# Hybrid decoder step: mixer tiles in pieces of 384, 320 and 352 tokens, weight slices laid out by parity of k

## What is computed

```
h = rmsnorm(x, g1) * (1 + scale1) + shift1;   z = h @ w_in         (mLSTM and GLA heads, gates)
y = (sigmoid(g_a) * ha + sigmoid(g_b) * hb) @ w_out;   x = x + gate1 * y
h2 = rmsnorm(x, g2) * (1 + scale2) + shift2
x = x + gate2 * ((silu(h2 @ w_gate) * (h2 @ w_up)) @ w_down)
```

## Time and profile before

| | |
|---|---|
| median of 3 runs | 1861.24 us (1857.82 to 1863.58) |
| the profiled execution, its own time | 1861.35 us |
| its span | 1859.5 us |
| TensorE matmuls | 14,443, busy 1822.0 us (98%) |
| TensorE weight loads | 14,443, busy 1741.6 us (94%) |
| VectorE, ScalarE, GpSimd busy | 57%, 37%, 39% |

### The profile page before, as it was taken

One profiled execution on the slowest core, in us unless ns is written; L12 is line 12 of the kernel. 1 busy time (PEld: TensorE's weight loads), 2 busy tenths in 40 slices (PEclk: granted clock), 3 DMA queues, 4 the chain that ended last, 5 costly groups with the idle time before them and its releaser, 6 DMA issues.

```text
span 1859.5 us, 35897 instructions
## 1 busy us (share of the span) xinstructions
PE 1822.0 (98%) x14443; PEld 1741.6 (94%) x14443; DVE 1062.4 (57%) x1886; ACT 682.3 (37%) x1401; POOL 728.6 (39%) x631
## 2 busy tenths in 40 slices
PE   7999999999999999999999999999999999999998
PEld 4899999999999999999998999989999999999998
DVE  6841645415464154541465688885675667566656
ACT  4533423334243343432435544223223223322337
POOL 4222332323333133322343773244345444544545
PEclk8999999999999999999999999999999999999999
DMA  9232222322223123222242742111112111111212
GB/s 319 103 105 57 78 86 69 118 63 82 81 69 123 53 83 90 71 87 88 83 139 84 226 120 63 46 46 47 47 46 63 29 58 58 58 35 47 69 46 94
DMA packets 182637, 154.77 MB, mean 83 GB/s; under 512 B 10325, under 2 KB 163093, under 8 KB 181961
## 3 DMA queue, kind: packets, MB, share of 16 engines
q1 hardware_dynamic: 182170, 152.27, 27.0%
q10 hardware_dynamic: 302, 0.22, 0.0%
HBM read 130.96 MB, written 21.50 MB: 82 GB/s over the span
## 4 chain that ended last, share of the span: by engine, by line
PE 83%; DVE 8%; issue 4%; POOL 2%; ACT 2%; DMA 0%; ACTq 0%; DVEq 0%; POOLq 0%; SPq 0%
PE bank L1013 28%; PE bank L2312 20%; PE bank L2281 11%; PE bank L1035 10%; PE bank L2179 2%; PE bank L1182 2%; PE bank L1184 1%; PE bank L1187 1%; PE bank L1225 1%; POOL mix L1498 1%; DVE y_rows L2926 1%; DVE x_t L2960 1%; PE bank L1160 1%; DVE y_rows L2745 1%; PE bank L339 1%
## 5 line engine op out<-in xcount | busy, mean ns | idle before, releaser
L1441 POOL TENSOR_TENSOR w_lo<-w_raw,w_hi 128x512 fp32r<-128x512 f32 x128 | 191.2, 1494 | 575.8 <-ACT w_hi L1240 575.8
L1013 PE MATMUL bank<-h_hi,w_hi 128*128 128x352 f32 x1152 | 246.7, 336 | 0.3 <-ACT w_hi L1240 0.3
L1013 PE MATMUL bank<-h_hi,w_lo 128*128 128x352 f32 x1152 | 232.6, 324 | 1.4 <-POOL w_lo L1441 1.4
L1013 PE MATMUL bank<-h_lo,w_hi 128*128 128x352 f32 x1152 | 232.1, 323 | 0.0
L2611 POOL TENSOR_TENSOR f_lo<-w_raw,f_hi 128x512 fp32r<-128x512 f32 x107 | 145.0, 1360 | 194.7 <-ACT f_hi L2376 194.7
L1013 PEld LDWEIGHTS bank<-h_hi,w_hi 128*128 128x128 f32 x1152 | 190.7, 189 | 14.6 <-issue 11.2
L2611 POOL TENSOR_TENSOR w_lo<-w_raw,w_hi 128x512 fp32r<-128x512 f32 x107 | 143.5, 1347 | 151.7 <-ACT w_hi L2376 151.7
L1013 PEld LDWEIGHTS bank<-h_hi,w_lo 128*128 128x128 f32 x1152 | 192.8, 188 | 3.7 <-POOL w_lo L1441 3.7
L1013 PEld LDWEIGHTS bank<-h_lo,w_hi 128*128 128x128 f32 x1152 | 193.2, 188 | 0.0
L2960 DVE SCALAR_TENSOR_TENSOR x_t<-bank,ada,x_t 128x352 f32<-128x352 f32 (+1 forms) x288 | 156.1, 568 | 55.5 <-PE bank L2281 38.8
L1240 ACT ACTIVATE w_hi<-w_raw 128x512 fp32r<-128x512 f32 x128 | 80.2, 626 | 107.3 <-PE bank L1013 69.8
(11 more groups left out here) (546 smaller groups left out, 4129.8 us busy)
## 6 DMA issues: line engine op xcount, KB each, us to landing
w_raw<-in_w_in SPq DMA_DIRECT2D x128, 256.0 KB, 3.0
w_ada_tile<-in_w_ada SPq DMA_DIRECT2D x32, 512.0 KB, 4.0
w_raw<-in_w_out SPq DMA_DIRECT2D x48, 256.0 KB, 2.8
w_raw<-in_w_ffn_gate SPq DMA_DIRECT2D x44, 256.0 KB, 3.0
w_raw<-in_w_ffn_up SPq DMA_DIRECT2D x44, 256.0 KB, 2.9
w_raw<-in_w_ffn_down SPq DMA_DIRECT2D x44, 256.0 KB, 2.9
w_ada_ring<-in_w_ada SPq DMA_DIRECT2D x10, 512.0 KB, 9.1
x_scratch<-x_turned_rows SPq DMA_DIRECT2D x1, 4224.0 KB, 16.3
```

The source lines that it names most:

```text
L1013: last = pe.matmul(g.ps[b][:, 0:n], x[:, s, k, :], y[:, 4 * h + k, c0:c0 + n], start=(h == 0 and k == 0 and m == 0), stop=(h == 1 and k == ...
L1441: pool.tensor_tensor(Wl[:, s], raw[:, r], Wh[:, s].bitcast(F32), ALU.subtract).then_inc(s_lo, 1)
```

## The change

1. In the mixer phase and in the first tile, the pieces of a tile are tokens 0 to 384, 384 to 704 and 704 to 1056: widths 384, 320 and 352. Their number and the sum of the widths stay. The later phase keeps 352 and 264.
2. `h_hi` and `h_lo` move by 32 bytes, so that they start at 0 mod 256.
3. The weight buffers are laid out anew. Slices with odd k lie in a second plane, 1,056 words behind that of the even ones, which is 128 mod 256. The four half buffers (high 0, high 1, low 0, low 1) lie 260 words apart, which is 16 bytes mod 256. ScalarE and GpSimd write each half as two planes of 256 words, through views of the same 512 elements.
4. For value tiles, the two column halves of one k lie next to each other in the plane of that k, so 256 columns are still streamed in one run.

With this, the distance in the mixer's `h` tiles is the same for every k: 32, 48, 64 or 80, by the half buffer that is loaded. In the value tiles it is 224, 208, 192 or 176.

```
+CUT = (0, 384, 704, T)
+ODD = 8 * P + 32
+def by_parity(w):
+    return w.rearrange("p (a b) c -> p a b c", b=2)
+def halves_of_columns(w):
+    return w.rearrange("p a b c -> p b a c")
+def slice_k(w, k):
+    return w[:, k // 2, k % 2, :]
...
         def span(c):
-            return c * PC, PC
+            return CUT[c], CUT[c + 1] - CUT[c]
...
-                        last = pe.matmul(g.ps[b][:, 0:n], x[:, s, k, :], y[:, 4 * h + k, c0:c0 + n],
+                        last = pe.matmul(g.ps[b][:, 0:n], slice_k(x[:, s], k), y[:, 4 * h + k, c0:c0 + n],
...
-                                             by_two(y[:, s])[:, k, :], start=...
+                                             y[:, s, :, k, :].rearrange("p a c -> p (a c)"), start=...
...
-                act.activation(Wh[:, s], raw[:, r], ACT.Copy).then_inc(s_hi, 1)
+                to = halves_of_columns(Wh[:, s]) if TILES[w][l][0] == "v" else Wh[:, s]
+                act.activation(to, by_parity(raw[:, r]), ACT.Copy).then_inc(s_hi, 1)
...
-                pool.tensor_tensor(Wl[:, s], raw[:, r], Wh[:, s].bitcast(F32), ALU.subtract).then_inc(s_lo, 1)
+                lo, hi = Wl[:, s], Wh[:, s]
+                if TILES[w][l][0] == "v":
+                    lo, hi = halves_of_columns(lo), halves_of_columns(hi)
+                pool.tensor_tensor(lo, by_parity(raw[:, r]), hi.bitcast(F32), ALU.subtract).then_inc(s_lo, 1)
...
-                                last = pe.matmul(g.ps[bnk][:, 0:n], x(s)[:, kk, :], y[:, 4 * h + kk, c0:c0 + n],
+                                last = pe.matmul(g.ps[bnk][:, 0:n], slice_k(x(s), kk), y[:, 4 * h + kk, c0:c0 + n],
...
-        sb("before_h", [P, 24])
+        sb("before_h", [P, 32])
...
-        sb("behind_h", [P, 8])
...
-        g.Wh = sb("w_hi", [P, 2, 4, P], F32R)
-        g.Wl = sb("w_lo", [P, 2, 4, P], F32R)
+        apart = lambda x: x[:, :, 0:4 * (2 * P + 4)].rearrange("p b (n r) -> p n b r", n=4)[:, :, :, 0:2 * P]
+        halves_at = lambda x, lo: apart(x)[:, 2 * lo:2 * lo + 2].rearrange("p s b (a c) -> p s a b c", a=2)
+        wx = sb("w_by_parity", [P, 2, ODD], F32R)
+        g.Wh, g.Wl = halves_at(wx, 0), halves_at(wx, 1)
...
-        W2 = (sb("f_hi", [P, 2, 4, P], F32R), sb("f_lo", [P, 2, 4, P], F32R))
-        g.rest = sb("rest_of_v_a", [P, NT * VX - 2 * D])
+        fx = sb("f_by_parity", [P, 2, ODD], F32R)
+        W2 = halves_at(fx, 0), halves_at(fx, 1)
+        g.rest = sb("rest_of_v_a", [P, NT * VX - 2 * ODD])
```

More of the change, by code:

```diff
@@ L267, in _ @@
                 pool.wait_ge(g.s_hi, n + 1)
-                pool.tensor_tensor(g.Wl[:, n], g.raw[:, n], g.Wh[:, n].bitcast(F32), ALU.subtract).then_inc(g.s_lo, 1)
+                pool.tensor_tensor(g.Wl[:, n], by_parity(g.raw[:, n]), g.Wh[:, n].bitcast(F32), ALU.subtract).then_inc(g.s_lo, 1)
         @block.tensor
@@ L338, in first_upper @@
                             pe.wait_ge(g.s_hsh, h + 1)
-                        pe.matmul(g.ps[c][:, 0:PC], w[:, h, k % 4, :], g.Hh[:, k, c * PC:(c + 1) * PC],
+                        pe.matmul(g.ps[c][:, 0:CUT[c + 1] - CUT[c]], slice_k(w[:, h], k % 4), g.Hh[:, k, CUT[c]:CUT[c + 1]],
                                   start=(k == 0 and m == 0), stop=False)
@@ L348, in first_lower @@
                         pe.wait_ge(g.s_hsl, h + 1)
-                    last = pe.matmul(g.ps[c][:, 0:PC], g.Wh[:, h, k % 4, :], g.Hl[:, k, c * PC:(c + 1) * PC],
+                    last = pe.matmul(g.ps[c][:, 0:CUT[c + 1] - CUT[c]], slice_k(g.Wh[:, h], k % 4), g.Hl[:, k, CUT[c]:CUT[c + 1]],
                                      start=False, stop=(k == KC - 1))
@@ L443, in weight @@
                 act.wait_ge(g.s_w[n], 48)
-                act.activation(g.Wh[:, n], g.raw[:, n], ACT.Copy).then_inc(g.s_hi, 1)
+                act.activation(g.Wh[:, n], by_parity(g.raw[:, n]), ACT.Copy).then_inc(g.s_hi, 1)
             partial(0)
@@ L784, in out_hi @@
                 act.wait_ge(s_used, MIX_HALVES + n - 3)
-            act.activation(g.W(0, out_slot(n)), raw[:, out_slot(n)], ACT.Copy).then_inc(g.f_hi, 1)
+            act.activation(g.W(0, out_slot(n)), by_parity(raw[:, out_slot(n)]), ACT.Copy).then_inc(g.f_hi, 1)
         def out_lo(pool, n):
             pool.wait_ge(g.f_hi, n + 1)
-            pool.tensor_tensor(g.W(1, out_slot(n)), raw[:, out_slot(n)], g.W(0, out_slot(n)).bitcast(F32), ALU.subtract).then_inc(g.f_lo, 1)
+            pool.tensor_tensor(g.W(1, out_slot(n)), by_parity(raw[:, out_slot(n)]), g.W(0, out_slot(n)).bitcast(F32), ALU.subtract).then_inc(g.f_lo, 1)
         def mix_hi(act, m):
@@ L1035, in mm_values @@
                             last = pe.matmul(g.ps[b][:, t % 2 * DV:(t % 2 + 1) * DV], x[:, 2 * n + k, t * P:(t + 1) * P],
-                                             by_two(y[:, s])[:, k, :], start=(n == 0 and k == 0 and m == 0 and t % 2 == 0),
+                                             y[:, s, :, k, :].rearrange("p a c -> p (a c)"), start=(n == 0 and k == 0 and m == 0 and t % 2 == 0),
                                              stop=(n == 3 and k == 1 and m == 2 and t % 2 == 1))
@@ L2228, in first_group @@
                             for kk in range(4):
-                                last = pe.matmul(g.ps[bnk][:, 0:PC], x(s)[:, kk, :], y[:, 4 * h + kk, 0:PC],
+                                last = pe.matmul(g.ps[bnk][:, 0:PC], slice_k(x(s), kk), y[:, 4 * h + kk, 0:PC],
                                                  start=(h == 0 and kk == 0 and m == 0), stop=(h == 1 and kk == 3 and m == 2))
@@ L2280, in half_piece @@
                         for m, (x, y) in enumerate(((Wh, Ah), (Wh, Al), (Wl, Ah))):
-                            last = pe.matmul(g.ps[bnk][:, 0:w], x(s)[:, r // 3, :], y[:, f, c0:c0 + w],
+                            last = pe.matmul(g.ps[bnk][:, 0:w], slice_k(x(s), r // 3), y[:, f, c0:c0 + w],
                                              start=(f == 0 and m == 0), stop=(f == 1 and m == 2))
@@ L2311, in seven @@
                             for kk in range(4):
-                                last = pe.matmul(g.ps[bnk][:, 0:HQ], x(s)[:, kk, :], BLOCK[block][kk][y][:, q * HQ:(q + 1) * HQ],
+                                last = pe.matmul(g.ps[bnk][:, 0:HQ], slice_k(x(s), kk), BLOCK[block][kk][y][:, q * HQ:(q + 1) * HQ],
                                                  start=(m == 0 and kk == 0), stop=(m == 2 and kk == 3))
@@ L2375, in hi @@
                 wait(act, s_used, n - (RING - 1))
-                act.activation(Wh(s), made_of(n), ACT.Copy).then_inc(s_hi, 1)
+                act.activation(Wh(s), by_parity(made_of(n)), ACT.Copy).then_inc(s_hi, 1)
             def t_hi(*which):
@@ L2610, in lo @@
                 wait(pool, s_used, n - (RING - 1))
-                pool.tensor_tensor(Wl(s), made_of(n), Wh(s).bitcast(F32), ALU.subtract).then_inc(s_lo, 1)
+                pool.tensor_tensor(Wl(s), by_parity(made_of(n)), Wh(s).bitcast(F32), ALU.subtract).then_inc(s_lo, 1)
             def mix_rest_lo(m):
```

## The result

The changed kernel takes 1864.49 us in the median of 22 runs (1861.72 to 1866.95), the kernel before 1861.00 us in 22 runs beside them (1857.82 to 1867.77). The ratio is 1.0021, 95% interval 1.0014 to 1.0028: slower by 0.21%, 3.5 us. By the bound of 0.3% this is "no change", by the interval a small loss. It lies in the range of 1820 to 1875, and 15 us above the forecast. The profiled execution took 1865.32 us, its span 1863.5.

The account below looks back on a forecast made before the run. It took the number of TensorE matmuls times their spacing to bound the kernel. Terms of 9.0 us (384 and 320 columns) and 3.1 (value tiles), 12.1 off 1861.35, gave 1849 us, 0.65% faster, range 1820 to 1875.

Parts of the forecast that it names:

- What bounds the kernel: Whole kernel: TensorE, busy for 98% of the span, sets the time as the number of matmuls times their spacing.
- 384 and 320 columns: Mixer `h` tiles, 2,304 matmuls: excess settles at 10.0 ns in place of 13.9, 9.0 us off.
- Value tiles: 1,536 matmuls: the tight spacing comes more often, excess 8.8 ns in place of 10.8, 3.1 us off.
- A distance that no longer alternates: Mixer and value tiles: every matmul of a run starts from what the last left; no separate size beside 9.0 and 3.1 us.
- Third pieces and the later phase: 352 pieces in mixer, output projection, plain tiles and down projection, plus seven-product tiles: other distances, counted as nothing.
- Casts and evacuations: ScalarE's cast and GpSimd's subtraction into two planes, and piece 0's later evacuation: no cost counted.
- The slower one: Rival, 352 and 256 tiles: the layout before already has the best distance; 15 us lost, 1876 us, chance 0.25.
- the classes of 264 columns: Seven-product tiles: mean excess 8.3, 11.2 or 12.5 ns by distance class, used to price the slower case.
- Its signs: For the slower case: line 1013 above 162 ns in the mean and the down projection above 161.
- No change: Rival, whole kernel: how a run begins decides its spacing, not addresses; 1861 us within 0.3%, chance 0.22.
- All tight: Rival: fixed distance alone brings tight spacing to all 352 pieces too; 66 us, 1795 to 1811 us, chance 0.11.
- The ports and the floor: Two skill rules: independent read ports, so the change does nothing; N/2.4 plus about 2.5 ns, so 352 takes 149.2 ns.

Follow-up runs that it names:

- experiment 1: Probe with TensorE alone, not a changed kernel: 32 equal matmuls for each of six lengths and 16 distances; 352 columns had 13.7 ns of excess in the mean.
- experiment 2: The kernel before with pieces of 384, 320 and 352 and nothing else changed: 1858.22 against 1860.11 us, ratio 0.9989.
- the probe: TensorE-only tiles in the mixer's order, ten pairs of layout and place, each behind eight lead-ins; old layout with 384, 320, 352 at place 192: 14.0 ns.
- planes alone: The changed kernel with pieces of 352, activations at 224 mod 256 and no 16-byte steps: 1861.01 us, ratio 0.9997.
- the probe of tiles: TensorE-only probe of whole tiles in three layouts and 16 places; value tiles in the old layout had 7.8 ns at 64 and 7.5 at 192.
- Experiments 3 and 4: First, the changed kernel with pieces of 352: 1862.96 us, 1.0015. Second, the kernel before with only `h` moved by 32 bytes: 1865.80 us, 1.0029.
- the probe of kinds: TensorE-only probe of one-pass float32, the same with 32-column loads, two-byte operands and plain float32; at 352 columns one-pass has 13.2 ns of excess, two-byte 2.5.
- experiment 12: The changed kernel with planes, no 16-byte steps and place 112, profiled again: second execution 1860.18 us; with pieces of 352, 1861.32 us, ratio 0.9999.

## Why the prediction was wrong

**What bounds the kernel** was read rightly: the loss is in the spacing of matmuls, and TensorE's busy time grew by 6.6 us. Two details were not. "At the full clock in all but the first slice" took a 9 in the page for 1.00, where the windows 960 to 980 and 1240 to 1255 us of the same trace show 0.91 and 0.89. And waits aren't a fixed addend: they fell as the products slowed.

**384 and 320 columns, -9.0 us: this step failed.** It took the two lengths to settle at 10.0 ns because the value tiles' 256 columns show 6.7 and 13.3, and all three are multiples of 64 words. Measured: (15.81 + 13.78)/2 = 14.8 ns. The low values of 256 go with its being short (experiment 1: means of 11.8, 13.4, 13.7, 15.3 and 18.2 ns for 256, 320, 352, 384 and 512 columns). In experiment 2 384 columns have 1.3 ns more than 352 had and 320 only 0.3 less, so the cut gains nothing: 14.0 ns in the kernel, 14.0 in the probe.

**Value tiles, -3.1 us: failed as well.** 10.57 ns instead of 8.8. The tight spacing was taken to follow from a distance that is the same for both k; with planes alone, which give that, the value tiles stand at 10.1. The working's count of 48 tight, 96 loose and 48 mixed was right for the kernel before, and it is by what ran before that the last 48 differ. Here the probe of tiles is no guide either: it has 7.5 at place 192 in the old layout, tight all through, where the kernel before shows both levels and 10.5 in the mean.

**A distance that no longer alternates** was the reason behind both. Planes alone give exactly that, and the mixer stands at 14.7 ns against 13.8.

**Third pieces and the later phase, 0: mis-sized.** 352 at other places costs 0.7 ns in the mixer (0.8 us), 0.8 in the output projection and plain tiles (0.8 us) and 0.9 in the down projection (1.4 us). That none of it would be lost was a guess for want of a row. The seven-product tiles at 0 were right (11.70 and 11.72 ns).

**Casts and evacuations, 0: right.** ScalarE's cast went from 626 to 627 ns, GpSimd's subtraction from 1,494 to 1,466; the waits for low parts did not grow (7.4 and 5.9 us).

**The rivals.** The slower one had the mechanism: the old places are better ones, and the change gives them up. Experiments 3 and 4 show it alone, +0.15% and +0.29%. Its size was a third: 0.9, 0.1 and 0.9 ns in `h` tiles, value tiles and down projection, where the classes of 264 columns said 1.8, 2.4 and 2.1. The classes don't carry over to other lengths and orders. Its signs, above 162 and above 161 ns, were missed: the means are 161.4 and 160.7. "No change" has the size, and its reason is half right: what ran before moves a single piece by 2.4 ns and the end of a value tile between 6.7 and 13.3, but over a whole `h` tile it averages out, and there the places matter by up to 3 ns. "All tight" is excluded: no whole `h` tile in any layout or place came under about 12 ns.

**The ports and the floor.** The Trainium skill, SBUF — State Buffer, section "Who interferes with whom", has TensorE's ports independent and TensorE never waiting. By it a place would cost nothing. With TensorE alone a tile's excess goes from 12.3 to 15.4 ns by where the two operands lie, so for one-pass float32 the runs don't agree. That it is the two ports that meet isn't shown: with a narrow load that stays in place, the stream's start alone moves 352 columns between 10.0 and 13.4 ns. The Trainium skill, TensorE: Matmul & The Clock Gate, section "Wait — 56ns, not 53.3ns?", has N/2.4 plus about 2.5 ns. Two-byte matmuls agree to the tenth (149.2 ns for 352); one-pass float32 doesn't, at 160.

**Open.** What in TensorE makes the excess, and the rule by which place, length, order and the work before set it, weren't found. So why the old places are better than the new ones stays open; the runs show that they are. Why TensorE's clock is granted less in some executions than in others wasn't tried either.

## What to carry to other kernels

A spacing seen in one shape (256 columns) doesn't carry to another (384) because both share a divisor; take a row of the same length, or a probe of the very order, before pricing it. Where operands lie in SBUF is worth up to 3 ns of 160 for one-pass float32 products, it repeats within some tenths of a ns over a whole tile, and a probe of one tile agreed within 0.3 ns with nine of ten kernels' `h` tiles (not with value tiles): try the places there, and read from the final addresses that the kernel has the place meant. Below 0.3%, compare the slope of the starts over long stretches and look at each run's granted clock: single executions differ by 1 to 5 us in steps, and those looked at were mostly the clock's. And before leaving out long spacings as waits, look whether they are waits.

## What was not expected of the hardware

- One-pass float32 matmuls have 11 to 18 ns over N/2.4 in the mean from 256 to 512 columns, often locked at 6.7, 10.0, 13.3 or 20.0 ns, thus at multiples of 8 cycles of 2.4 GHz; two-byte ones have 2.5 ns at every length.
- At the same distance of load and stream, 512 columns had 13.3 or 16.8 ns by whether both started at an even or odd multiple of 16 bytes.
- In the probe of kinds the granted clock stood at a half for 20 us, twice, with one-pass matmuls back to back (the 5s in its clock row). It fell during those of 96 columns, behind those of 64, and rose during those of 192; those of 128 and 160 columns between them start 213 ns apart.
- Of two executions of one program (experiment 12), one has a granted clock of 0.83 from 90 to 100 us and of 0.89 from 1240 to 1255, the other 1.00 in both, but 0.58 from 1837 to 1848, right after a stretch at 1.00 with TensorE busy for 11.74 us of 13.
- A plain float32 matmul of 352 columns takes 591.7 ns, 3.7 times a one-pass one at 160. It is two rows of the trace, each 2N/2.4 + 2.5 ns.
